# A mixture-of-experts kernel with split weights: the subtractions for the lower parts move from GpSimd to VectorE

## What is computed

```
a = jnp.einsum('td,thkd->thk', h, u_tab[expert]).astype(jnp.float32)
coef = (g * jax.nn.gelu(a)).astype(h.dtype)
return jnp.einsum('thk,thkd->td', coef, v_tab[expert])
```

## The kernel before, in words

| phase | TensorE | gate groups in it |
|---|---|---|
| 1 | up of quarter 1 | for quarter 0 |
| 2 | down of quarter 0 | for quarter 1 |
| 3 | up of quarter 2 | none |
| 4 | down of quarter 1 | for quarter 2 |
| 5 | up of quarter 3 | none |
| 6 | down of quarter 2 | for quarter 3 |
| 7 | down of quarter 3 | none |

## Time and profile before

### The profile page before, as it was taken

The page is one execution under the profiler, slowest core; times in us unless marked ns, Lnnn a source line. Parts: engine busy times, 40 slices in busy tenths (PEclk is TensorE's granted clock), DMA queues, the critical chain, the costliest instruction groups (busy, mean ns, idle before and its releaser), DMA issues.

```text
span 2986.6 us, 55057 instructions
## 1 busy us (share of the span) xinstructions
PE 2622.3 (88%) x21835; PEld 2379.8 (80%) x21835; DVE 1962.9 (66%) x2664; ACT 810.3 (27%) x1066; POOL 1369.3 (46%) x572
## 2 busy tenths in 40 slices
PE   8898997878799889888999989978788998898887
PEld 3687877778798789878877878778677997898787
DVE  1122599997946991994154125999989458929941
ACT  1303213231252144113201132122312531342132
POOL 0413204554476567556521032045544764675565
PEclk9999998998999999999996589989989998999999
DMA  4333332222243334323653033323222432343332
GB/s 165 124 120 113 127 133 107 100 99 86 100 155 127 100 125 159 109 98 127 193 174 97 3 110 127 130 98 110 92 92 100 154 129 100 113 162 107 107 120 84
DMA packets 51284, 349.51 MB, mean 117 GB/s; under 512 B 6112, under 2 KB 6128, under 8 KB 11408
## 3 DMA queue, kind: packets, MB, share of 16 engines
q1 hardware_dynamic: 44928, 324.16, 31.7%
q0 software_dynamic: 6192, 22.95, 2.7%
HBM read 342.83 MB, written 4.26 MB: 116 GB/s over the span
## 4 chain that ended last, share of the span: by engine, by line
PE 58%; DVE 22%; issue 16%; POOL 3%; DVEq 1%; ACT 1%; DMA 0%; POOLq 0%; ACTq 0%
DVE hots L1301 14%; PE ps L611 9%; PE ps L601 8%; PE ps L612 8%; PE ps L617 8%; PE ps L585 4%; PE ps L511 3%; POOL w_lo L372 2%; PE ps L534 2%; DVE hots L1294 2%; PE ps L789 2%; PE ps L466 2%; DVE C_lo L1343 2%; PE ps L467 2%; PE ps L468 2%
## 5 line engine op out<-in xcount | busy, mean ns | idle before, releaser
L372 POOL TENSOR_TENSOR w_lo<-ring,w_hi 128x1024 fp32r<-128x1024 f32 x448 | 1196.2, 2670 | 1063.3 <-PE ps L612 821.5
L947 ACT ACTIVATE w_hi<-ring 128x1024 fp32r<-128x1024 f32 x448 | 473.1, 1057 | 960.7 <-PE ps L612 928.8
L611 PE MATMUL ps<-C_hi,w_hi 128*128 128x288 f32 x2048 | 655.7, 320 | 43.7 <-DVE C_lo L1343 29.9
L617 PE MATMUL ps<-C_hi,w_lo 128*128 128x288 f32 x2048 | 629.2, 307 | 0.0
L612 PE MATMUL ps<-C_lo,w_hi 128*128 128x288 f32 x2048 | 624.7, 305 | 0.0
L1301 DVE TENSOR_TENSOR hots<-hots,parts 128x768 bf16<-128x768 bf16 x304 | 569.2, 1873 | 0.0
L611 PE MATMUL ps<-h_hi,w_hi 128*128 128x288 f32 x1536 | 472.3, 307 | 11.6 <-POOL w_lo L372 8.0
L612 PE MATMUL ps<-h_lo,w_hi 128*128 128x288 f32 x1536 | 460.2, 300 | 0.0
L617 PE MATMUL ps<-h_hi,w_lo 128*128 128x288 f32 x1536 | 459.5, 299 | 0.0
L611 PEld LDWEIGHTS ps<-C_hi,w_hi 128*128 128x128 f32 x2048 | 409.4, 200 | 50.5 <-issue 28.5
L1297 DVE TENSOR_TENSOR hots<-iota,halves 128x1024 bf16<-128x1024 bf16 x304 | 421.0, 1385 | 0.0
(11 more groups left out here) (211 smaller groups left out, 2688.1 us busy)
## 6 DMA issues: line engine op xcount, KB each, us to landing
ring<-in_U SPq DMA_DIRECT2D x128, 1024.0 KB, 4.8
ring<-in_V SPq DMA_DIRECT2D x128, 1024.0 KB, 4.8
ring<-in_peer_q SPq DMA_DIRECT2D x16, 1024.0 KB, 4.7
ring<-in_w_in_v SPq DMA_DIRECT2D x8, 1024.0 KB, 6.7
ring<-in_w_in_u SPq DMA_DIRECT2D x8, 1024.0 KB, 4.7
ring<-in_w_out SPq DMA_DIRECT2D x8, 1024.0 KB, 4.7
work<-in_cache POOLq DMA_DIRECT2D x8, 512.0 KB, 5.4
big<-in_cache POOLq DMA_DIRECT2D x8, 512.0 KB, 7.1
```

What stands on the lines that cost most here:

```text
L372: pool.tensor_tensor(w_lo[:, k % LO_SLOTS, :], ring[:, k // 2, (k % 2) * HBLK:(k % 2 + 1) * HBLK], w_hi[:, k % HI_SLOTS, :], ALU.subtract) ...
L611: one = pe.matmul(out, w_hi[:, h % HI_SLOTS, at], hi, start=start, stop=False)
L617: return pe.matmul(out, w_lo[:, h % LO_SLOTS, at], hi, start=False, stop=stop)
L947: act.activation(w_hi[:, k % HI_SLOTS, :], ring[:, bl % R, (k % 2) * HBLK:(k % 2 + 1) * HBLK], ACT.Copy).then_inc(hi_made, 1)
```

## The change

The 448 subtractions for w_lo leave GpSimd's program. `lower_parts` becomes `lower_h`, which keeps only h's lower part. DVE gets them in `lower_half(n)`, with the same waits and the same counter. The first is issued before the slots are built; within a phase, `lower_half` for the next half stands at the head of each half's turn.

To place them, DVE's loops are written out: `phase` walks through the 32 halves, and for each issues the next half's subtraction, chunks of C_lo where they are due, the gate groups that TensorE does in that half, and every fourth half the addition. C_lo is spread: in phase 2 four chunks before the first half and two in each of the first two; in phases 3 and 5 one after each of halves 1 to 8; phase 7 is as phase 2. Two other things change with it: `one_hot_group` is no longer issued for the two groups behind a quarter's last (304 issues become 288), and the two groups ahead of a quarter are issued at the end of the phase before.

```
-            def lower_parts(layer):
+            def lower_h(layer):
...
                 pool.tensor_tensor(h_lo[:], hT[:], h_hi[:], ALU.subtract).then_inc(h_lo_made, 1)
...
-                        pool.wait_ge(hi_made, n + 1 if it is None else it * (2 * R) + (n + 1))
-                        if n >= LO_SLOTS or it is not None:
-                            begun = n - LO_SLOTS + 2
-                            pool.wait_ge(halves_begun, begun if it is None else it * (2 * R) + begun)
-                        pool.tensor_tensor(w_lo[:, k % LO_SLOTS, :], ring[:, k // 2, (k % 2) * HBLK:(k % 2 + 1) * HBLK],
-                                           w_hi[:, k % HI_SLOTS, :], ALU.subtract).then_inc(lo_made, 1)
...
+                def lower_half(n):
+
+                    dve.wait_ge(hi_made, layer * SPLIT + n + 1)
+                    if layer * SPLIT + n >= LO_SLOTS:
+                        dve.wait_ge(halves_begun, layer * SPLIT + n - LO_SLOTS + 2)
+                    k = n % (2 * R)
+                    dve.tensor_tensor(w_lo[:, n % LO_SLOTS, :], ring[:, k // 2, (k % 2) * HBLK:(k % 2 + 1) * HBLK],
+                                      w_hi[:, n % HI_SLOTS, :], ALU.subtract).then_inc(lo_made, 1)
+
+                lower_half(0)
                 dve.memset(slots[:, :, T:3 * P], 0.0)
...
+                    dve.tensor_tensor(dst, dst, src, ALU.mult).then_inc(gate_free, 1)
+                    if j + LEAD < NGG:
+                        one_hot_group(q, j + LEAD)
...
+                def phase(nth, gates=None, split=None, down=None, next_gates=None):
+
+                    if gates is not None:
+                        dve.wait_ge(act_free, A0[f"U{layer}"] + (gates + 1) * EQ)
+                    if split is not None:
+                        dve.wait_ge(gate_free, (layer * NQ + split + 1) * NGG + CREDIT)
+                        if down is not None:
+                            lower_C(split, range(4))
+                    for h in range(EQ):
+                        if nth * EQ + h + 1 < SPLIT:
+                            lower_half(nth * EQ + h + 1)
+                        if split is not None and down is not None and h < 2:
+                            lower_C(split, (4 + 2 * h, 5 + 2 * h))
+                        if split is not None and down is None and 1 <= h <= len(CCHUNKS):
+                            lower_C(split, (h - 1,))
+                        if gates is not None:
+                            it, k = h // 16, h % 16
+                            for j in range(due(k, 16, gates), due(k + 1, 16, gates)):
+                                gate_group(gates, it * GR + j)
+                        if down is not None and h % 4 == 3:
+                            add_partial(down, h // 4)
+                    if next_gates is not None:
+                        for j in range(LEAD):
+                            one_hot_group(next_gates, j)
+
+                for j in range(LEAD):
+                    one_hot_group(0, j)
+                phase(0, gates=0, next_gates=1)
+                phase(1, gates=1, split=0, down=0)
+                phase(2, split=1, next_gates=2)
+                phase(3, gates=2, down=1)
+                phase(4, split=2, next_gates=3)
+                phase(5, gates=3, down=2)
+                phase(6, split=3, down=3)
```

More of the change, by code:

```diff
@@ L357, in _ @@
             pool.dma_start(o["a_v_sample"], v[0:NSAMP, 2, :]).then_inc(av_saved, 16)
-            def lower_parts(layer):
+            def lower_h(layer):
                 pool.wait_ge(h_hi_made, layer + 1)
                 pool.tensor_tensor(h_lo[:], hT[:], h_hi[:], ALU.subtract).then_inc(h_lo_made, 1)
-                def ring_round(it):
-                    for k in range(2 * R):
-                        n = layer * SPLIT + k
-                        pool.wait_ge(hi_made, n + 1 if it is None else it * (2 * R) + (n + 1))
-                        if n >= LO_SLOTS or it is not None:
-                            begun = n - LO_SLOTS + 2
-                            pool.wait_ge(halves_begun, begun if it is None else it * (2 * R) + begun)
-                        pool.tensor_tensor(w_lo[:, k % LO_SLOTS, :], ring[:, k // 2, (k % 2) * HBLK:(k % 2 + 1) * HBLK],
-                                           w_hi[:, k % HI_SLOTS, :], ALU.subtract).then_inc(lo_made, 1)
-                ring_round(None)
-                with pool.Fori(1, SPLIT // (2 * R)) as it:
-                    ring_round(it)
             early_lower_parts(16)
-            lower_parts(0)
+            lower_h(0)
             pool.wait_ge(x_ready, 2)
@@ L405, in _ @@
             early_lower_parts(32)
-            lower_parts(1)
+            lower_h(1)
             for c in (0, DC // 2):
@@ L579, in gate_groups @@
                     for j in range(due(done, of, q), due(done + 1, of, q)):
-                        pe.wait_ge(hot_ready, it * GR + (nth * (NGG + LEAD) + j + 1))
+                        pe.wait_ge(hot_ready, it * GR + (nth * NGG + j + 1))
                         pe.wait_ge(gate_free, it * GR + (nth * NGG + j - 1 + CREDIT))
@@ L1284, in peer, with one_hot_group @@
                         link(dve.tensor_tensor(slots[:, 2, :], slots[:, 2, :], parts[:, c, :], ALU.subtract))
-                def one_hot_group(q, j, it):
+                def one_hot_group(q, j):
                     s = j % RH
-                    tok = j * GT if it is None else it * (GR * GT) + j * GT
-                    before = (layer * NQ + q) * (NGG + LEAD) + j
+                    before = (layer * NQ + q) * NGG + j
                     if before:
-                        dve.wait_ge(hot_ready, before if it is None else it * GR + before)
+                        dve.wait_ge(hot_ready, before)
+                    toks = slice(j * GT, (j + 1) * GT)
@@ L1294, in one_hot_group @@
                     step(dve.tensor_tensor(here2, iota16[:, q * EQ:(q + 1) * EQ].unsqueeze(1).broadcast_to((P, GT, EQ)),
-                                           halves[:, 1, bass.ds(tok, GT)].unsqueeze(2).broadcast_to((P, GT, EQ)),
-                                           ALU.is_equal))
+                                           halves[:, 1, toks].unsqueeze(2).broadcast_to((P, GT, EQ)), ALU.is_equal))
                     dve.tensor_tensor(hot1[:, s], iota16[:].unsqueeze(1).broadcast_to((P, GT, NK)),
-                                      halves[:, 0, bass.ds(tok, GT)].unsqueeze(2).broadcast_to((P, GT, NK)),
@@ L1299, in one_hot_group @@
-                                      ALU.is_equal)
+                                      halves[:, 0, toks].unsqueeze(2).broadcast_to((P, GT, NK)), ALU.is_equal)
                     last_step()
                     dve.tensor_tensor(hot2[:, s], here2.unsqueeze(1).broadcast_to((P, 3, GT, EQ)),
-                                      parts[:, :, bass.ds(tok, GT)].unsqueeze(3).broadcast_to((P, 3, GT, EQ)),
+                                      parts[:, :, toks].unsqueeze(3).broadcast_to((P, 3, GT, EQ)),
@@ L1303, in one_hot_group @@
                                       ALU.mult).then_inc(hot_ready, 1)
[L1305 to L1336, removed]
@@ L1338, in lower_C, with gate_group @@
-                def lower_C(q):
-                    dve.wait_ge(gate_free, (layer * NQ + q + 1) * NGG + CREDIT)
-                    for k, (e0, e1) in enumerate(CCHUNKS):
+                def gate_group(q, j):
+                    dve.wait_ge(gate_full, (layer * NQ + q) * NGG + j + 1)
+                    dst = C[:, q % 2, :, j * GT:(j + 1) * GT]
+                    src = ps[:, 6 + j % 2, 0:GT * EQ].rearrange("p (t e) -> p e t", t=GT)
+                    dve.tensor_tensor(dst, dst, src, ALU.mult).then_inc(gate_free, 1)
+                    if j + LEAD < NGG:
+                        one_hot_group(q, j + LEAD)
@@ L1342, in lower_C @@
+                def lower_C(q, chunks):
+                    for k in chunks:
+                        e0, e1 = CCHUNKS[k]
                         dve.wait_ge(C_hi_made, (layer * NQ + q) * len(CCHUNKS) + k + 1)
@@ L1344, in lower_C, with add_partial @@
                                           ALU.subtract).then_inc(C_lo_made, 1)
[L1346 to L1349, removed]
+                def add_partial(q, dc):
+                    dve.wait_ge(dve_full, D0[f"V{layer}"] + q * DC + dc + 1)
+                    dst = xT[:, dc:dc + 1, :]
+                    dve.tensor_tensor(dst, dst, ps[:, 4 + dc % 2:5 + dc % 2, 0:T], ALU.add).then_inc(dve_free, 1)
```

## The result

The changed kernel takes 2745.99 us (median of four, 2742.07 to 2751.76) against 2985.31 us: a ratio of 0.9202, 95% interval 0.9185 to 0.9218. It is faster by 8.0%, 239 us. The prediction was 2738 us in a range of 2685 to 2815. The profiled execution of the changed kernel is the fastest of its four (2742.07 us), and its span is compared with the span before, 2986.6 us.

What follows compares the result with a forecast made beforehand. DVE, delayed by GpSimd's subtractions, was taken to bound the gate phases. Saving 250 us there and 20 in phases without gates, less 24 for friction, gave 2741 from 2986.6, or 2738 us after 2.2 for the median; range 2685 to 2815.

Steps and rivals of the forecast that it cites:

- The mutual delay: In gate phases, DVE instructions with two SBUF inputs and GpSimd subtractions exclude one another; 2.2 us of DVE delay per overlapping subtraction.
- The subtraction's price: Each of the 448 w_lo subtractions added to DVE was taken at 1.15 us, with 1.32 us as the upper end.
- G3: Fourth phase of each layer, the third with gates; predicted 133.7 us for 161.9 and 166.8 before.
- G1: First phase of each layer, with gates; predicted 135.2 us for 161.9 before.
- G2: Second phase of each layer, with gates; predicted 146 us for 182.2 and 181.2 before.
- G4: Sixth phase of each layer, the fourth with gates; predicted 136.3 us for 168.7 and 168.0 before.
- uneven turns: Halves with one or two gate groups or a waiting addition on DVE; guessed at 3 us per gate phase, 24 in all.
- Phases without gates: Third, fifth and seventh phases of each layer; predicted to save 3.5, 3.5 and 3 us, 20 in both layers.
- N1 and N2: Third and fifth phases of each layer, without gates; predicted to save 3.5 us each.
- That turns bind: Rival, 18%: DVE's single order makes late halves block groups and late groups block w_lo; about 2875 us, or 2805.
- TensorE as the bound: Rival, 10%: gate phases fall to TensorE's 126 us plus the same starts and tails; about 2660 us.
- The slower rival: Rival, 3%: DVE's long rows have another cause than GpSimd, so the subtractions come on top; about 3240 us.

## Why the prediction was right

The mechanism was right, and each large term was near. That the total came so close is in part luck: by the spans 246.3 us were saved for 246 predicted, and three errors cancel in it: the sum counted 13 us too much for the gate phases, 4 too little for the others, and nothing for 9 us that were saved outside the phases.

*The mutual delay.* This carried the sum and was right in kind and size. The one-hot rows came down to 0.415 (mean over 288), 1.215 and 0.948 us, and thirty extra GpSimd subtractions a layer brought it back at 127 / 60 = 2.1 us each, for the 2.2 read from the earlier trace rows.

*The subtraction's price.* 1.219 us long, for the 1.224 of the earlier trace rows; spaced 1.14 us (481.54 to 482.68 in the rows below), for the 1.15 taken; 1.17 by doing it twice.

```profile
480.67 0.94 DVE L1295 TENSOR_TENSOR hots<-hots,parts 128x768 bf16<-128x768 bf16 x1
481.54 1.21 DVE L1264 TENSOR_TENSOR w_lo<-ring,w_hi 128x1024 fp32r<-128x1024 f32 x1
482.68 0.41 DVE L1304 TENSOR_TENSOR big<-big,ps 128x256 f32<-128x256 f32 x1
```

*The phases.* G3 was 134.3 us in both layers for 133.7 predicted. The others were longer than their sums: G1 138.5 and 140.7 for 135.2, G2 152.0 and 150.5 for 146, G4 147.7 and 141.5 for 136.3. Against the 24 us set aside for uneven turns, the eight exceed their sums by 1139.5 - 1102 = 37.5 us. That term was mis-sized by some 13 us: against 3 us a phase G4 is over by 10.6 us in the two layers, G2 by 4.5 and G1 by 2.8, and G3 is under by 4.8. In G4 the backlog that was to carry DVE over the stretch without groups in the phase's middle was gone. DVE and then TensorE in G4's middle:

```profile
1169.17 1.22 DVE L1264 TENSOR_TENSOR w_lo<-ring,w_hi 128x1024 fp32r<-128x1024 f32 x1 [1.01 <-PE ps L597]
1176.96 0.42 DVE L1304 TENSOR_TENSOR big<-big,ps 128x256 f32<-128x256 f32 x1 [6.56 <-PE ps L570]
```

```profile
1168.56 0.38 PE L596 MATMUL ps<-C_hi,w_hi 128*128 128x288 f32 x1 [2.75 <-DVE xT L1320]
1171.60 0.61 PE L602 MATMUL ps<-C_hi,w_lo 128*128 128x288 f32 x1 [2.54 <-issue]
```

TensorE waits 2.75 us for an addition that stands behind two groups on DVE, then stands 2.54 us with nothing that the profile shows to wait for, and DVE in turn idles 6.56 us for TensorE. My sum had this in G2 (1 us) and not in G4. What the 2.54 us are stays open; they come in the first half of the loop's second round on TensorE, in layer 0 only. After them TensorE's clock was lower for 4 us (windows of this trace, columns as above):

```profile
1166.00:1171.60 5.60, 0.50 (x2) 0.30 (x2) 3.38 (x4) 1.06 (x1) 0.00 (x0) 0.77 0.09 13
1171.60:1175.70 4.10, 4.10 (x17) 4.10 (x18) 0.00 (x0) 0.00 (x0) 0.00 (x0) 0.50 0.69 246
```

TensorE was busy for 0.50 us of the first 5.60, and then ran at 0.50, the 1.2 GHz level. Layer 0's G4 is 6.2 us longer than layer 1's: the gap of 2.5 us, and 3.7 us more of busy time on TensorE (134.53 against 130.81) at a granted clock of 0.95 against 0.99, while its waits for w_lo and for the addition are alike (9.3 and 9.4 us). No term of the sum had the clock. What it cost the other phases isn't separated by any run here.

*A sign of being wrong.* The prediction named DVE's idle time before the multiply within gate phases, while TensorE waits. It did appear, in small: DVE idled 31.6 us in 19 waits ahead of L1304, the 6.56 us above among them. That DVE works "without a gap" held for G3 (133.41 of 134.30 us) and not for layer 0's G2 (140.28 of 152.00) and G4 (135.29 of 147.70).

*The stall ahead of G2.* Kept, as said: 3.73 us for the 3.88 of the earlier trace rows.

*Phases without gates.* The six windows add up to 647.0 us before and 620.6 after, 26.4 less. The last window before reaches to 2966.0, 2.1 us past its phase's last matmul, so 24.3 us were saved for 20: once nothing delays C_lo and w_lo, N1 and N2 have no wait at all.

*Not in the sum:* the remaining 246.3 - 213.1 - 24.3 = 8.9 us lie outside the phases, 6.6 between the layers' stretches (497.9 us before, 491.3 after) and 2.2 ahead of the first (468.5 against 466.3). The first subtractions of a layer on GpSimd had also delayed DVE's work ahead of the first gate group. Three instructions that took 2.75 us there (the first line, of before) take 0.59 (the second, after):

```profile
455.69 2.75 DVE L1268 TENSOR_TENSOR work<-work 128x128 f32<-128x128 f32 x3
```

```profile
455.56 0.59 DVE L1253 TENSOR_TENSOR work<-work 128x128 f32<-128x128 f32 x3
```

In layer 1 the same three took 2.75 us, and a cast beside the next GpSimd subtraction was long too (DVE, then GpSimd, of before):

```profile
1956.06 2.43 DVE L1282 CAST parts<-slots 128x384 bf16<-128x384 f32 x1
```

```profile
1955.89 2.39 POOL L372 TENSOR_TENSOR w_lo<-ring,w_hi 128x1024 fp32r<-128x1024 f32 x1 [3.77 <-PE ps L612]
```

The same cast, after, is never above 0.361 us. It has one SBUF operand, so the delay isn't confined to instructions with two, the only ones that the prediction counted. No run isolates it. From DVE's last reduction before these rows to the first gate group, layer 1 takes 4.1 us less than before (11.5 for 15.7); the other 2.5 us between the stretches are not traced.

*Slips in the working.* DVE's busy time in gate phases before was put at 158 to 167 us beside G1; layer 1's G3 has 153.38 of 166.80 us, 13 us short of saturation. L1297's spacing is 1.14 us in the earlier trace rows, not 1.13, so the lower end for the subtractions is -3 us and not -5. Subtractions at 1.32 us are given as 44 us more in one place and 38 in another; by 256 x 0.17 it is 44, and the forecast's own range should reach 6 us further. The 0.9 us for the first subtraction stand in G1's sum but lie ahead of its window. None of these moves the forecast by more than 2 us.

*The rivals.* That turns bind was given 137 us for one turn in five; another order takes back some 9 to 11. TensorE as the bound did not come: it needs 128 us, not 126, and half-width subtractions were needed to reach it. The slower rival fell with the two runs of extra GpSimd work.

## What to carry to other kernels

Before work is moved to GpSimd to relieve DVE, or left there, look for DVE instructions of one line and shape that appear with two durations (here those with two SBUF operands, and one cast): if the longer one exceeds the shorter by about a GpSimd instruction, the two engines are not parallel there, and 1.2 us on DVE can cost less than 2.4 us on GpSimd beside it. An engine that is busy all the time by the windows may be waiting inside its instructions; the minimum of a row against its mean says how much. Once two engines are near balance (133 against 128 us here), price the work of both, and expect the phases to exceed the sum: by 3% over the eight here (37 us), and by 11.4 us in the worst, layer 0's G4, where a gap without a known cause and the lower clock have a part.

## What was not expected of the hardware

A DVE cast with one SBUF operand took 2.43 us beside a GpSimd subtraction, for 0.36 otherwise. GpSimd's memset of 128x1024 f32 took 0.96 us and delayed nothing on DVE, while a subtraction of that size took 2.41 us alone and 3.3 us beside DVE. The granted clock rose in gate phases as TensorE waited less: 0.96 and 0.91 in layer 0's G1 and G2 before, 0.99 and 0.97 after; in the run with doubled subtractions, where TensorE waits more, it was 0.90 in both.
